# Two side loads issued later and five pieces of TensorE work put in another order, in a two-block network on one core

## The chip, the cores and the metric

The kernel runs on one core of one Trainium2 chip. The metric is the time of one execution in microseconds (us). Three runs of the kernel before took 1758.71, 1763.52 and 1771.0 us, so the median is 1763.52 us.

## The reference, cut to what matters

256 tokens of width 1024 pass through two networks one after the other, all in 32-bit floats.

```
# first network, 2 layers: mixer, then a mixture of 16 experts (each takes 32 tokens)
h = rms_norm(x) * (1 + scale) + shift            # scale, shift, gate = silu(c) @ ada_w + ada_b
layer 0 mixer: proj = h @ fc_w_in                # 1024 -> 1536: 512 Fourier, 1024 gated convolution
               y_f = real(fft2(...)); y_c = silu(layer_norm(conv31(u_v * sigmoid(u_g))))
               y = concat(y_f, y_c) @ fc_w_out
layer 1 mixer: windowed attention, 16 heads, rotary positions
x = x + gate * y;  x = x + gate * experts(...)
x = rms_norm(x, final_norm_g)

# second network, 1 layer, with 256 context tokens beside the 256 latent ones
proj_l, proj_c = hl @ w_in, hc @ w_in
a = differential attention over context and latent keys (4 heads, both 128-row blocks)
b = neighbourhood attention with a bias table rpb (4 heads)
p = pooling mix;  h = hyena mix (two long convolutions)
xl = xl + gate * (concat(a, b, p, h) @ w_out)
xl = xl + gate2 * moe(...)                       # 16 experts, top 2 inside one group
out = rmsnorm(xl, final_g)
```

## The kernel before, in words

There is one instruction stream for each engine, written out by hand in the order of execution, and semaphores between them. The two 128-token tiles (T = 0, 1) lie on the 128 partitions.

**Weights.** SyncE (SP) streams all weights in pieces of 1 MB, in the order of use, into a ring of 8 slots (`load`, line 320 on, profile line L322; pairs of pieces at L333). Before it issues piece n it waits (`place_free`) until TensorE has counted up `piece_used` far enough that the slot is free. TensorE waits in `loaded(...)` for the piece to land.

**Side loads.** GpSimd's queue (`@block.gpsimd`, L2107 on) loads small constants in a fixed order, each behind a semaphore wait. After the ninth weight piece is used it issues, without a further wait: the first gate bias (L2111), the Fourier tables (L2113), the router weights (L2114), the row constants (L2116), the first network's last gain (L2117, 512 KB in SBUF, read at L1632 of the second block's start), and four copies of the bias table from DRAM to DRAM (L2119, in rows of 127 floats; read back in `pool_block2` at L991, after the wait for `rpb_copied`). Then come the gate bias of the next site (`load_gate_bias(1)`, L2129), the filter constants, gate bias 2, `window` and `positions` (L2138, L2139), `load_gate_bias(3)`, and `pool_block2`.

**Opening.** TensorE works through the first modulation blocks (`ada_block`), the convolution half of `fc_w_in`, then the two Fourier half pieces (`P_FC_FOURIER`), the Fourier transforms, `ada_block(3..5)`, and half of the output projection. VectorE meanwhile runs the 31 taps of the convolution (L2850) and then signals `conv_ready`, for which TensorE waits before it sums the convolution over channels.

**Experts** of the first network are two loops of 16 experts (`experts`), 12 pieces each. Between them lies the attention stage (`pe_attention`): six pieces of `attn_w_qkv` (`P_QKV`), then modulation blocks 9 to 13 and the heads.

**Second mixer** (`pe_block2`, L1024 on). `context(q)` projects the context tokens with piece q of `w_in` into PSUM banks 4 and 5; after q = 3 it signals `ctx_ps`. `transposed_norm(4, 4, 0)` turns the normalised latent tokens into banks 0 to 3; VectorE and ScalarE scale them into `hT`, and TensorE waits for that in `h_ready(4)` before the latent projection. After that comes a loop over 12 head groups (8 "diff", 4 "near"; `N2` = 12). In step g TensorE does the scores of group g+1, then a block of other work chosen by g, then waits for the probabilities of group g-1, transposes them (`turned_probs`, 4 instructions, L2150), waits until ScalarE has copied them out of PSUM (`pT2_ready`), and multiplies them with the values (`weighted`). A "near" group has a second half that is transposed and copied after the first. The other work includes `keys_values(T, bank)` in steps 2 and 3 (8 rows k of the projection of keys and values, PSUM bank 5 or 7), two gate rows and four parts of the output projection (`out_part`) in steps 11 and 12.

ScalarE's own order in steps 2 and 3 is fixed in `act_block2`: first the exponentials, then a wait for `in_b_ps` and the copy of keys and values out of PSUM (L1536, L1537), then the wait for the transposed probabilities (`pT2_ps`) and their copy. GpSimd waits for `ctx_ps` before it loads the bias table (L982). A last loop of 17 experts of 6 pieces follows, and the final normalisation.

Of the kernel before, what the change touches and what calls it, by code (L numbers as in the profile page):

```python
# [29 lines left out]
P = 128  # L30
D = 1024
KD = D // P
# [32 lines left out]
P_QKV = P_ADA_8 + 4  # L65
# [122 lines left out]
def build(nc, A, WHERE):  # L188

    with ExitStack() as ctx:  # L190
# [5 lines left out]
        def S(name):  # L196

            if name not in sems:
                sems[name] = ctx.enter_context(nc.semaphore(name))
            return sems[name]  # L200
# [14 lines left out]
        rpb_rows = nc.dram_tensor("rpb_rows", (4, 7, 64, 128), F32, kind="Internal").ap()  # L215


        ps = ctx.enter_context(nc.psum_tensor("ps", [P, 8, 512], F32))
# [8 lines left out]
        rows = sb("rows", [P, width("rows")])  # L227
# [128 lines left out]
        def read(g):  # L356

            return ORDER.index(g) + 1
# [665 lines left out]
        def pe_block2(pe, mm, tr, transposed_norm, h_ready, gate_row, ada_piece, ada_block):  # L1024
# [11 lines left out]
                    last.then_inc(S("ctx_ps"), 1)  # L1036

            pe.wait_ge(S("gate_added"), 4)
            for q in range(4):
                context(q)  # L1040
            transposed_norm(4, 4, 0)
            h_ready(4)
            for T in range(NT):
                for q in range(4):
# [21 lines left out]
                if f % 2:  # L1066
                    last.then_inc(S("hy_ps"), 1)

            def keys_values(T, bank):
                for k in range(KD):  # L1070
                    last = mm(ps[:, bank, :], hT[:, k, P * T:P * T + P], wide_in(4 + k // 2)[:, k % 2, 0:512],
                              k == 0, k == KD - 1)
                last.then_inc(S("in_b_ps"), 1)

            def pool_in(bank):
                for T in range(NT):
# [47 lines left out]
            def out_part(T, i):  # L1124
                if T == 0:
                    loaded(pe, P_OUT2 + i)
                w = slot(P_OUT2 + i).rearrange("p (k f) -> p k f", k=2)
                for kk in range(2):
                    for n in range(2):
                        last = mm(ps[:, 2 * T + n, :], ycat2[:, 2 * OUT2_ORDER[i] + kk, P * T:P * T + P],  # L1130
                                  w[:, kk, 512 * n:512 * n + 512], i + kk == 0, i == 3 and kk == 1)
                if T == 1:
                    last.then_inc(S("piece_used"), 1)
                elif i == 3:
                    last.then_inc(S("out_ps"), 1)
# [73 lines left out]
            for g in range(N2 + 1):  # L1209
                if g + 1 < N2:  # L1210
                    scores(g + 1)
                if g == 0:
                    feature(2, 5)
                    feature(3, 5)
                if g == 1:
                    pe.wait_ge(S("hy_in"), 1)
                    feature(4, 7)
                if g == 2:
                    pe.wait_ge(S("hy_in"), 2)
                    keys_values(0, 5)  # L1220
                if g == 3:
                    pe.wait_ge(S("hy_in"), 3)
                    keys_values(1, 7)
                if g == 4:
                    pe.wait_ge(S("in_b_act"), 1)
                    four(5, [pla[:, T, 256 + P * i:384 + P * i] for i in range(2) for T in range(NT)])
                    pe.wait_ge(S("in_b_act"), 2)
                    pe.wait_ge(S("b2_const"), 64)
                    long_conv(0, "turn")
                if g == 5:  # L1230
                    pe.wait_ge(S("qk_ready"), 5)
                    near_keys(1, 5)
                    long_conv(0, "forward")
                if g == 6:
                    pe.wait_ge(S("y_spec"), 1)
                    pool_in(5)
                if g == 7:
                    pe.wait_ge(S("pool_m"), 16)
                    pe.wait_ge(S("in_b_dve"), 1)
                    for i in range(4):  # L1240
                        o = 64 * (i % 2)
                        for T in range(NT):
                            last = mm(ps[o:o + 64, 5, SEQ * (i // 2):SEQ * (i // 2) + SEQ], pu[:, T, 64 * i:64 * i + 64],
                                      pool_m[:, T, i, :], i < 2 and T == 0, T == NT - 1)
                    last.then_inc(S("pool_ps"), 1)
                    long_conv(1, "turn")
                if g == 8:
                    long_conv(1, "forward")
                if g == 9:
                    long_conv(1, "back")  # L1250
                if g == 10:
                    pe.wait_ge(S("oa_ready"), 1)
                    pe.wait_ge(S("hy_out"), 1)
                    for T in range(NT):
                        for i in range(2):
                            last = tr(ps[:, 7, SEQ * i + P * T:SEQ * i + P * T + P],
                                      oa[:, T].rearrange("p h d -> p (h d)")[:, P * i:P * i + P])
                    last.then_inc(S("oaT_ps"), 1)
                if g == 11:
                    pe.wait_ge(S("row_copied"), read(14))  # L1260
                    mm(ps[:, 5, :], wide[:, 1, 0, :], gate_rows[:, 4, :], True, True)
                    pe.wait_ge(S("ycat2_ready"), 1)
                    mm(ps[:, 7, :], wide[:, 1, 1, :], gate_rows[:, 4, :], True, True).then_inc(S("gate_ps"), 1)
                    pe.wait_ge(S("exps2_ready"), 22)
                    out_part(0, 0)
                    out_part(0, 1)
                if g == 12:
                    pe.wait_ge(S("o2_ready"), 10)
                    out_part(0, 2)
                    out_part(0, 3)  # L1270
                if g:
                    near_group = A_GROUPS[g - 1][0] == "near"
                    pe.wait_ge(S("probs2_ready"), g)
                    n = turned_probs(g - 1, 0)
                    if g == 1:
                        feature(5, 7)
                    if g == 4:
                        pe.wait_ge(S("qk_ready"), 4)
                        near_keys(0, 5)
                    if g == 6:  # L1280
                        long_conv(0, "back")
                    if g == 7:
                        pe.wait_ge(S("pooled"), 1)
                        for i in range(4):
                            o = 64 * (i % 2)
                            last = mm(ps[o:o + 64, 5, SEQ * (i // 2):SEQ * (i // 2) + SEQ], pool_w[o:o + 64, i // 2, :],
                                      pp[o:o + 64, i // 2, :], i < 2, True)
                        last.then_inc(S("pool_ps"), 1)
                    if g == 9:
                        ada_block(14)  # L1290
                    if g == 12:
                        pe.wait_ge(S("exps2_ready"), 24)
                        out_part(1, 0)
                        x_turned(0, (5, 7))
                    pe.wait_ge(S("pT2_ready"), n)
                    if near_group:
                        turned_probs(g - 1, 1)
                    weighted(g - 1, 0)
                    if g == 12:
                        logits(0, 5)  # L1300
                        out_part(1, 1)
                    if near_group:
                        pe.wait_ge(S("pT2_ready"), n + 1)
                        weighted(g - 1, 1)
# [803 lines left out]
        def _(pool):  # L2108
# [5 lines left out]
            pool.dma_start(routers[:, :, :, :].rearrange("p l (n t) e -> p l n t e", n=2), A["routers"].rearrange("l (n p t) e -> p l n t e", p=P, t=4))\  # L2114
                .then_inc(S("routers"), 16)
            pool.dma_start(rows[:, :], A["rows"].broadcast_to([P, rows.shape[1]])).then_inc(S("routers"), 16)  # L2116
            pool.dma_start(last_gain[:, :], A["final_norm_g"].broadcast_to([P, D])).then_inc(S("last_gain"), 16)  # L2117
            for h in range(NA_H):
                pool.dma_start(rpb_rows[h, :, :, 0:127],  # L2119
                               A["rpb"][h, 4:11].unsqueeze(1).broadcast_to([7, 64, 127]))\  # L2120
                    .then_inc(S("rpb_copied"), 16)
            ada_biases = [A["ada_b"][l, j] for l in range(2) for j in range(2)]
            gate_bias = [b[2 * D:3 * D] for b in ada_biases]
            gate_bias += [A["ada_b_2"][0, 2 * D:3 * D], A["ada_b_2"][0, 5 * D:6 * D]]
# [1 line left out]
            def load_gate_bias(k):  # L2126

                pool.wait_ge(S("x_ready"), 2 * k)
                pool.dma_start(gate[:, :], gate_bias[k].rearrange("(a f) -> a f", a=1).broadcast_to([P, D]))\  # L2129
                    .then_inc(S("gate_bias"), 16)  # L2130
# [6 lines left out]
            load_gate_bias(2)  # L2137
            pool.dma_start(window.rearrange("p a b -> p (a b)"), A["window"]).then_inc(S("phase_const"), 16)  # L2138
            pool.dma_start(posi, A["positions"]).then_inc(S("phase_const"), 16)  # L2139
            load_gate_bias(3)  # L2140
            pool_block2(pool, load_gate_bias)

# [932 lines left out]
```

## Time and profile before

| | |
|---|---|
| runs | 1758.71, 1763.52, 1771.0 us |
| median | 1763.52 us |
| profiled execution, its own time | 1758.08 us |
| its span, first to last instruction | 1756.3 us |
| granted TensorE clock, mean | 0.898 of full speed |
| busy: TensorE matmul, VectorE, ScalarE, GpSimd | 77%, 25%, 13%, 1% |
| DMA | 640 MB, mean 364 GB/s |

"L" with a number is a line of the kernel; several operations share a helper's line (all ordinary matmuls are L2147, transposes L2150, ScalarE's work L2518), so a group is told apart by its time, tiles and shape. A time is that from the start of the span. Idle time in square brackets is that of the engine just before the group, and behind the arrow is what ended it. A 32-bit matmul shows as two instructions.

### The profile page before, as it was taken

Reading aid. Unit: us, or ns where it says so; the run is one execution under the profiler, and the core shown is the slowest. Engines: PE = TensorE matmul, PEld = TensorE weight load, DVE = VectorE, ACT = ScalarE, POOL = GpSimd, SP = SyncE. Lnnn points to the kernel's source line nnn. Section 1 sums busy time; section 2 is a strip of 40 time slices with the busy share of each in tenths; the row PEclk is TensorE's granted clock in tenths of the full one; section 3 lists DMA queues with packets and bytes.
Section 4 is the critical chain, followed back from the end, with each engine's and each line's share of the span. In section 5 each row is a group of like instructions: output and inputs, shape, how many; then the busy total and the mean of one; then the engine's idle time right before and its main releaser. Section 6 shows DMA issues by size and latency. Waiting matters only on the chain.

```text
span 1756.3 us, 25665 instructions
## 1 busy us (share of the span) xinstructions
PE 1355.8 (77%) x11264; PEld 736.3 (42%) x11264; DVE 439.8 (25%) x1014; ACT 223.2 (13%) x470; POOL 25.7 (1%) x46
## 2 busy tenths in 40 slices
PE   7999665666666579897766666655699888999997
PEld 4755332332323234553323333322346645655553
DVE  1674211013100024643101000000126465322122
ACT  2122000000000021531000000000112233100001
POOL 1000000000000000000000000000020000000000
PEclk9998888888888899998788787788899999999999
DMA  9999999999999997849999999999951325899996
GB/s 375 362 367 358 427 423 427 423 426 424 426 424 426 424 407 299 343 170 399 424 425 424 426 424 427 423 426 424 419 208 65 144 109 195 345 421 421 421 420 256
DMA packets 89484, 640.11 MB, mean 364 GB/s; under 512 B 8508, under 2 KB 8508, under 8 KB 43296
## 3 DMA queue, kind: packets, MB, share of 16 engines
q1 hardware_dynamic: 85712, 625.85, 86.8%
q0 software_dynamic: 3664, 12.64, 2.0%
q8 instruction: 90, 1.47, 0.3%
q14 instruction: 18, 0.15, 0.0%
HBM read 637.40 MB, written 1.96 MB: 364 GB/s over the span
## 4 chain that ended last, share of the span: by engine, by line
DMA 48%; PE 44%; DVE 5%; ACT 1%; issue 1%; SPq 0%; DVEq 0%; ACTq 0%
PE ps L2147 42%; DMA ring<-in_moe_w_up 31%; DMA ring<-in_moe_w_down 13%; PE ps L2150 2%; DMA ring<-in_fc_w_in 2%; DMA ring<-in_attn_w_qkv 1%; DMA ring<-in_moe_w 1%; DMA ring<-in_ada_w 1%; ACT work L2518 1%; DVE work L803 0%; SPq L322 0%; DVE work L2923 0%; DVE work L784 0%; DVE work L788 0%; ACT hT L2518 0%
## 5 line engine op out<-in xcount | busy, mean ns | idle before, releaser
L2147 PE MATMUL ps<-ring,work 128*32 128x256 f32 (+3 forms) x7696 | 754.7, 457 | 330.1 <-DMA ring<-in_moe_w_gate 151.1
L2147 PEld LDWEIGHTS ps<-ring,work 128*32 128x32 f32 (+2 forms) x7696 | 349.4, 131 | 714.9 <-issue 268.7
L2518 ACT ACTIVATE work<-ps 128x256 f32<-128x256 f32 (+3 forms) x171 | 79.0, 467 | 1213.9 <-PE ps L2147 1019.3
L2957 DVE TENSOR_TENSOR work<-work,ps 128x256 f32<-128x256 f32 x32 | 13.5, 421 | 622.3 <-ACT work L2518 622.3
L2147 PE MATMUL ps<-work 32*128 32x256 f32 (+7 forms) x1098 | 155.5, 447 | 10.0 <-ACT work L2518 6.6
L2147 PEld LDWEIGHTS ps<-work 32*128 32x128 f32 (+4 forms) x1098 | 89.2, 199 | 73.7 <-issue 58.5
L2147 PE MATMUL ps<-ring,hT 128*128 128x512 f32 (+1 forms) x224 | 92.3, 573 | 6.1 <-DMA ring<-in_attn_w_qkv 3.0
L2150 PE MATMUL ps<-const,work 128*128 128x128 f32 (+1 forms) x392 | 64.0, 294 | 13.2 <-DVE work L803 6.1
L2147 PE MATMUL ps<-ring,condT 128*32 128x512 f32 x560 | 71.4, 630 | 3.0 <-DMA ring<-in_ada_w 3.0
L2147 PE MATMUL ps<-hT,ring 128*128 128x256 f32 x288 | 67.4, 395 | 4.2 <-DMA ring<-in_fc_w_in 2.6
L2147 PE MATMUL ps<-work,xn 128*128 128x128 f32 (+2 forms) x448 | 66.6, 300 | 1.8 <-DVE work L1905 1.6
L2150 PEld LDWEIGHTS ps<-const,work 128*128 128x128 f32 (+1 forms) x392 | 46.6, 161 | 48.2 <-issue 23.1
L2147 PEld LDWEIGHTS ps<-ring,hT 128*128 128x128 f32 x224 | 43.3, 195 | 54.8 <-issue 49.4
L2147 PEld LDWEIGHTS ps<-hT,ring 128*128 128x128 f32 x288 | 56.4, 198 | 16.1 <-issue 4.7
L2147 PEld LDWEIGHTS ps<-work,xn 128*128 128x128 f32 x448 | 58.1, 191 | 9.2 <-issue 7.0
L2975 DVE TENSOR_TENSOR work<-ps,gate 128x256 f32<-128x256 f32 x32 | 13.6, 425 | 153.4 <-PE ps L2147 153.4
L2850 DVE SCALAR_TENSOR_TENSOR work<-work,cols 128x256 f32<-128x256 f32 x120 | 47.6, 477 | 0.0
L2518 ACT ACT_TABLE_LOAD x28 | 35.9, 1283 | 1.8 <-DVE condT L2706 1.4
L2147 PEld LDWEIGHTS ps<-ring,condT 128*32 128x32 f32 x560 | 16.9, 115 | 43.4 <-issue 36.2
L2518 ACT ACTIVATE work<-work 128x256 f32<-128x256 f32 (+7 forms) x55 | 27.4, 500 | 47.5 <-DVE work L1735 14.5
L1967 DVE TENSOR_TENSOR work<-work,ps 128x256 f32<-128x256 f32 x17 | 7.2, 421 | 92.2 <-PE ps L2147 92.1
L2942 DVE TENSOR_SCALAR work<-ps,gain,mod 128x128 f32<-128x128 f32 x56 | 19.1, 404 | 28.1 <-PE ps L2147 28.0
(305 smaller groups left out, 655.2 us busy)
## 6 DMA issues: line engine op xcount, KB each, us to landing
ring<-in_moe_w_up SPq DMA_DIRECT2D x64, 2048.0 KB, 17.8
ring<-in_moe_w_down SPq DMA_DIRECT2D x128, 1024.0 KB, 15.9
ring<-in_moe_w_gate SPq DMA_DIRECT2D x63, 2048.0 KB, 16.9
ring<-in_moe_w SPq DMA_DIRECT2D x102, 1024.0 KB, 10.9
ring<-in_ada_w SPq DMA_DIRECT2D x70, 1024.0 KB, 10.4
ring<-in_w_in SPq DMA_DIRECT2D x10, 1024.0 KB, 18.1
ring<-in_fc_w_in SPq DMA_DIRECT2D x6, 1024.0 KB, 15.8
ring<-in_attn_w_qkv SPq DMA_DIRECT2D x6, 1024.0 KB, 20.3
```

Of the source, the lines that this page charges most:

```text
L1967: v.tensor_tensor(hid3, act3, ps[:, 5, 0:SEQ], ALU.mult).then_inc(S("hid3_ready"), 1)
L2147: return pe.matmul(out, lhsT, rhs, start=start, stop=stop, skip_group_check=True)
L2150: return pe.matmul(out, in_, ident[0:n, 0:n], is_transpose=True, start=True, stop=True, skip_group_check=True)
L2518: return nc.scalar.activation(out, in_, f, **kw)
L2850: ins = v.scalar_tensor_tensor(cv[:, g, :], src, w, cv[:, g, :], op0=ALU.mult, op1=ALU.add)
L2942: v.tensor_scalar(xe[:, c % 2, j, :], ps[:, bank, P * (j % 4):P * (j % 4) + P], gain[:, site, j:j + 1], mod[:, 3 * site, j % 4, j // 4, 0: ...
L2957: v.tensor_tensor(hid, act, ps[:, 5, 0:SEQ], ALU.mult).then_inc(S("hid_ready"), 1)
L2975: v.tensor_tensor(ye, ps[:, 7, 0:SEQ], gate[:, 0:SEQ], ALU.mult).then_inc(S("ye_ready"), 1)
```

## The change

On GpSimd's queue the load of the first network's last gain and the four copies of the bias table are issued later: behind `positions`, after a new wait for the third `attn_w_qkv` piece to be used, and ahead of `load_gate_bias(3)`. On TensorE, `context(3)` stands behind the transposes of the latent tokens; the last row k of each `keys_values` stands behind the first transposes of its step; the first of the two gate rows stands in step 10 behind the transposes, not in step 11 ahead of them; and `out_part(0, 1)` stands in step 11 behind the transposes. ScalarE's and VectorE's programs are as before.

```diff
             pe.wait_ge(S("gate_added"), 4)
-            for q in range(4):
+            for q in range(3):
                 context(q)
             transposed_norm(4, 4, 0)
+            context(3)
             h_ready(4)
...
-            def keys_values(T, bank):
-                for k in range(KD):
+            def keys_values(T, bank, rows):
+                for k in rows:
                     last = mm(ps[:, bank, :], hT[:, k, P * T:P * T + P], wide_in(4 + k // 2)[:, k % 2, 0:512],
                               k == 0, k == KD - 1)
-                last.then_inc(S("in_b_ps"), 1)
+                if rows.stop == KD:
+                    last.then_inc(S("in_b_ps"), 1)
...
                 if g == 2:
                     pe.wait_ge(S("hy_in"), 2)
-                    keys_values(0, 5)
+                    keys_values(0, 5, range(KD - 1))
                 if g == 3:
                     pe.wait_ge(S("hy_in"), 3)
-                    keys_values(1, 7)
+                    keys_values(1, 7, range(KD - 1))
...
                 if g == 11:
-                    pe.wait_ge(S("row_copied"), read(14))
-                    mm(ps[:, 5, :], wide[:, 1, 0, :], gate_rows[:, 4, :], True, True)
                     pe.wait_ge(S("ycat2_ready"), 1)
                     mm(ps[:, 7, :], wide[:, 1, 1, :], gate_rows[:, 4, :], True, True).then_inc(S("gate_ps"), 1)
                     pe.wait_ge(S("exps2_ready"), 22)
                     out_part(0, 0)
-                    out_part(0, 1)
...
                     n = turned_probs(g - 1, 0)
                     if g == 1:
                         feature(5, 7)
+                    if g in (2, 3):
+                        keys_values(g - 2, 5 if g == 2 else 7, range(KD - 1, KD))
...
                     if g == 9:
                         ada_block(14)
+                    if g == 10:
+                        pe.wait_ge(S("row_copied"), read(14))
+                        mm(ps[:, 5, :], wide[:, 1, 0, :], gate_rows[:, 4, :], True, True)
+                    if g == 11:
+                        out_part(0, 1)
...
-            pool.dma_start(last_gain[:, :], A["final_norm_g"].broadcast_to([P, D])).then_inc(S("last_gain"), 16)
-            for h in range(NA_H):
-                pool.dma_start(rpb_rows[h, :, :, 0:127],
-                               A["rpb"][h, 4:11].unsqueeze(1).broadcast_to([7, 64, 127]))\
-                    .then_inc(S("rpb_copied"), 16)
...
             pool.dma_start(posi, A["positions"]).then_inc(S("phase_const"), 16)
+            pool.wait_ge(S("piece_used"), P_QKV + 3)
+            pool.dma_start(last_gain[:, :], A["final_norm_g"].broadcast_to([P, D])).then_inc(S("last_gain"), 16)
+            for h in range(NA_H):
+                pool.dma_start(rpb_rows[h, :, :, 0:127],
+                               A["rpb"][h, 4:11].unsqueeze(1).broadcast_to([7, 64, 127]))\
+                    .then_inc(S("rpb_copied"), 16)
             load_gate_bias(3)
```

## Rows read from the trace of the kernel before

**Rows 1.** The page: chain that ended last by line, and DMA share in 40 slices.

```profile
PE ps L2147 42%; DMA ring<-in_moe_w_up 31%; DMA ring<-in_moe_w_down 13%; PE ps L2150 2%; DMA ring<-in_fc_w_in 2%; DMA ring<-in_attn_w_qkv 1%; DMA ring<-in_moe_w 1%; DMA ring<-in_ada_w 1%; ACT work L2518 1%; DVE work L803 0%; SPq L322 0%; DVE work L2923 0%; DVE work L784 0%; DVE work L788 0%; ACT hT L2518 0%
...
DMA  9999999999999997849999999999951325899996
```

**Rows 2.** Chain of waits, opening: start us, length us, what.

```profile
37.73 27.38 DMA ring<-in_fc_w_in
```

**Rows 3.** Timeline of TensorE, opening: start us, length us, group, idle before it.

```profile
24.89 8.83 PE L2147 MATMUL ps<-hT,ring 128*128 128x256 f32 x32 [1.67 <-DVE hT L2731]
...
41.62 17.51 PE L2147 MATMUL ps<-hT,ring 128*128 128x256 f32 x80
...
65.25 15.74 PE L2147 MATMUL ps<-hT,ring 128*128 128x256 f32 x64 [2.55 <-DMA ring<-in_fc_w_in]
...
113.29 1.89 PE L2147 MATMUL ps<-work,const 128*128 128x256 f32 x8
```

**Rows 4.** Stretch; its length, TensorE busy; granted clock; DMA share; GB/s.

```profile
26.00:28.00 2.00, 2.00 (x6) 0.50 1.05 386
```

**Rows 5.** Timeline of VectorE, opening: the convolution and the signal behind it.

```profile
62.92 47.59 DVE L2850 SCALAR_TENSOR_TENSOR work<-work,cols 128x256 f32<-128x256 f32 x120
110.55 0.15 DVE L2855 COPY work<-work 128x1 f32<-128x1 f32 x1
```

**Rows 6.** DMA queues from 49 to 60 us: packets, MB, share of 16 engines.

```profile
q0 software_dynamic: 715, 1.41, 41.0%
```

**Rows 7.** The page's DMA issues of the moved loads: count, KB each, us to landing.

```profile
rpb_rows<-in_rpb POOLq DMA_DIRECT2D x4, 222.2 KB, 16.5
...
last_gain<-in_final_norm_g POOLq DMA_DIRECT2D x1, 512.0 KB, 12.6
```

**Rows 8.** Timeline of TensorE, attention stage, the six query, key and value pieces.

```profile
641.73 41.44 PE L2147 MATMUL ps<-ring,hT 128*128 128x512 f32 x96 [3.05 <-DMA ring<-in_attn_w_qkv]
```

**Rows 9.** Attention stage: stretch, TensorE busy, clock, DMA share, GB/s.

```profile
662.00:667.00 5.00, 5.00 (x13) 1.00 0.94 353
667.00:685.00 18.00, 18.00 (x58) 1.00 0.51 171
```

**Rows 10.** Timeline of TensorE, start of the second mixer.

```profile
1270.24 16.21 PE L2147 MATMUL ps<-ring,work 128*128 128x512 f32 x32
1286.29 2.09 PE L2150 MATMUL ps<-const,xn 128*128 128x128 f32 x16
1290.31 27.70 PE L2147 MATMUL ps<-ring,hT 128*128 128x512 f32 x64 [1.93 <-ACT hT L2518]
```

**Rows 11.** Timeline of VectorE: last normalised tile.

```profile
1279.95 0.75 DVE L2765 TENSOR_SCALAR xn<-x,small 128x1024 f32<-128x1024 f32 x1
```

**Rows 12.** Timeline of TensorE, step 2: transposes, then the weighted values.

```profile
1353.58 0.60 PE L2150 MATMUL ps<-const,work 128*128 128x128 f32 x4
1354.92 1.10 PE L2147 MATMUL ps<-work 128*128 128x64 f32 x8 [0.75 <-ACT work L2518]
```

**Rows 13.** Chain of waits, step 2: ScalarE's two copies.

```profile
1353.78 0.45 ACT work L2518
...
1354.27 0.61 ACT work L2518
```

**Rows 14.** Timeline of TensorE, steps 10 and 11.

```profile
1429.21 0.66 PE L2150 MATMUL ps<-const,work 128*128 128x128 f32 x4 [2.66 <-ACT work L2518]
...
1431.57 1.98 PE L2147 MATMUL ps<-gate_rows,const 128*128 128x512 f32 x4
1433.39 7.03 PE L2147 MATMUL ps<-ring,work 128*128 128x512 f32 x16
...
1441.60 0.66 PE L2150 MATMUL ps<-const,work 128*128 128x128 f32 x4 [0.75 <-ACT work L2518]
```

**Rows 15.** Timeline of ScalarE, step 9: the row of modulation block 14 copied.

```profile
1421.86 0.59 ACT L2518 ACTIVATE gate_rows<-ps 128x512 f32<-128x512 f32 x1
```

**Rows 16.** Timeline of VectorE: probabilities that step 11 transposes.

```profile
1428.97 1.23 DVE L1715 TENSOR_TENSOR work<-work 128x1024 f32<-128x1024 f32 x1
```

## The prediction

> **What bounds the kernel now.** I read the chain of waits first. By line it is 44% DMA of expert weights (31 and 13) and 42% TensorE matmuls [rows 1]: the two loops of experts of the first network wait for the weight stream, and the opening, the two mixers and the attention stage wait for TensorE. The DMA share over the span says the same: full in the loops, low in the second mixer [rows 1]. Between these stages the coupling is one of order only: the stream is at most 8 pieces ahead of TensorE, so when TensorE reaches the end of a stage earlier by some amount, the slots come free that much earlier and everything behind shifts. What the change wins or loses in a stage bound by TensorE therefore reaches the end in full, unless a second chain stands close behind. Both stages that it touches are of that kind, with one exception in each: in the opening a DMA piece is late once [rows 2], and in the second mixer TensorE waits several times for VectorE or ScalarE.
>
> **Opening: what leaves.** TensorE waits 2.55 us for a Fourier piece of the input projection, which took 27.38 us from issue to landing [rows 2, 3]. Then it runs its 64 instructions in 15.74 us; at the 17.51/80 = 0.219 us that the same form takes before, they would be 14.0 us, so the wait costs 1.7 us more by the clock. The moved loads are 512 KB and 4 x 222 KB, 1.43 MB [rows 7]. On the way of the late piece GpSimd's queue moved 1.41 MB from 49 to 60 us and took 41% of 11 us, 4.5 us of all engines [rows 6]. At the plain 386 GB/s of [rows 4] these bytes would be 3.7 us. Both are more than 2.55 us, so the piece lands in time: 2.55 + 1.7 = 4.25 us gone. The five issues themselves lie on a queue that nothing waits for here.
>
> **Opening: what is late next.** The convolution on VectorE does not depend on that piece. It starts at 62.92 and its signal comes at 110.55 + 0.15 = 110.70 us [rows 5]. TensorE asks for it at 113.29 [rows 3]; 4.25 us earlier is 109.04, so it stands for 1.7 us and leaves 113.29 - 110.70 = 2.6 us earlier than before. Such a stand has a price of its own. The nearest row is an idle of 1.67 us before 24.89: the 32 instructions behind it took 8.83 us instead of 7.0 [rows 3], and from 26 to 28 us the granted clock was 0.50, the 1.2 GHz level [rows 4]. Between no loss and this 1.8 us I take 1.8, since the length of the stand is the same. Opening: -2.6 + 1.8 = -0.8 us; ends -2.6, and +0.3 if a second slow stretch of the kind falls in.
>
> **Attention stage.** The third of six pieces is used at 641.73 + 41.44/2 = 662.4 us [rows 8]; then the five loads go out. GpSimd's next duty behind them is a gate bias that waits for the end of this stage, so nothing is queued up. On the DMA engines the loads need the 4.5 us of above. From 662 to 667 the share is 0.94, from 667 to 685 it is 0.51 [rows 9]: 0.3 + 8.8 = 9.1 us of all engines stand free. TensorE works through [rows 8, 9] with slots full ahead of it. Cost 0, hidden by a stream that waits for slots; with that cover gone it would be up to 4.5 us.
>
> **context(3).** A piece of context is 8 instructions at 27.70/64 = 0.433 us, 3.5 us [rows 10]. The transposes start at 1286.3 - 3.5 = 1282.8 instead; their input is there at 1279.95 + 0.75 = 1280.7 [rows 11]. VectorE and ScalarE then finish `hT` at 1290.3 - 3.5 = 1286.8, while context(3) runs until 1288.4. The 1.93 us of idle [rows 10] go: -1.9 us, and 0 at worst. The signal `ctx_ps` comes 2.1 us later; ScalarE's copies behind it are not asked for until the heads, and GpSimd's 16 loads of the bias table are wanted in step 2, some 60 us on. Cost 0.
>
> **keys_values, twice.** TensorE does the last row (2 instructions, 0.87 us) behind the transposes, so as to fill the 0.75 us in which it waits for ScalarE [rows 12]. But look at what ScalarE does in this gap: two copies, at 1353.78 and 1354.27 [rows 13]. The first is that of the keys and values, released by the end of `keys_values`, and stands ahead of the other in ScalarE's order, which the change leaves alone. Now that projection ends 0.45 to 0.60 us later, by the four transposes put ahead of it [rows 12], and ScalarE begins both copies that much later. Everything behind follows: +0.45 us in each of the two steps, +0.9 in sum, where the gap seems to promise -0.75 each. I take the loss, since the order of ScalarE's program leaves no other way; ends -1.5 and +1.2.
>
> **Gate row.** Four instructions of two rows hold 1433.39 - 1431.57 = 1.82 us [rows 14]; one row is 0.9. In step 10 it falls into an idle of 2.66 us [rows 14]. Its input was copied at 1421.86 + 0.59 = 1422.45 [rows 15], before that idle. -0.9 us; 0 at worst.
>
> **out_part(0, 1).** Half of 7.03 us, 3.5 us [rows 14], goes behind the transposes and covers the 0.75 us until the second half's transposes may start. The transposes then start at about 1440.2 - 0.9 - 3.5 = 1435.8; the probabilities are there at 1430.2 [rows 16]. -0.75 us; 0 at worst.
>
> **Sum.** -0.8 + 0 - 1.9 + 0.9 - 0.9 - 0.75 = -3.5 us. Against the profiled execution, 1758.08 us, that is 1754.6. The median of the runs lies 5.4 us above that execution; from 1763.5 the same sum gives 1760.0 us.
>
> **Rivals.**
> - **The stand at the convolution costs no clock.** For it: how often the clock falls behind an idle of this length is not fixed, one row is little. The opening gives -2.6 and the total is -5.3: 1758.2 us.
> - **keys_values gains as it looks.** That needs ScalarE's two copies not to be the limit; [rows 13] speak against it. Then -1.5 stands for +0.9 and the total is -5.9: 1757.6 us.
> - **The opening's change doesn't do what it says.** The late piece may be late by the weight queue's own backlog, with GpSimd's share lying elsewhere; 41% in the very stretch [rows 6] speaks against. Then the opening gives 0 and the total is -2.7: 1760.8 us.
> - **The side loads collide in the attention stage (slower).** While both queues have work the side loads held 41% of the engines [rows 6], so weight pieces land later than by their bytes. It decides at 9.1 us free [rows 9] against 4.5 needed: if the pieces for modulation blocks 9 and 10 land late, TensorE waits 4.5 us right behind 683 us and loses 1.8 us by the clock: +6.3 - 3.5 = +2.8, 1766.3 us. TensorE's stream without a DMA wait there and the free share speak against it. The Trainium skill (DMA: Bandwidth & Descriptors, Queues, rings and completion order) has each engine go round between the queues that have work, whatever is urgent, and (same page, Specifications) says that transfers under 512 bytes run below line rate; the table's rows are 508 bytes. By these two the loads would press harder on the weight pieces than their bytes say, in the opening as in the new place; the trace's 41% agrees with the first.
>
> **Chances.** Forecast as summed 0.4; no clock loss 0.2; keys_values gains 0.1; no effect in the opening 0.15; collision 0.12; the rest is something not seen. The predicted time is that of the forecast, 1760. The lowest mechanism is -2.6 - 1.9 - 1.5 - 0.9 - 0.75 = -7.7, 1755.9; the highest 1766.3. The three runs before lie from 4.8 below to 7.5 above their median, and a median of new runs can move by some 3 to 5 of that by itself: range 1751 to 1769. About 1% (17.6 us) is what a measurement of this kernel can tell from no change. Every case lies inside it, so within 1% gets 0.94, and 0.03 each side.
>
> **What would show it.** Opening: no DMA wait before the Fourier instructions, and these in 14.0 us; a new idle of about 1.7 us just before the sums over channels, ended by VectorE's signal, with the clock at 0.5 behind it or not. Attention: no DMA wait from 683 on. Second mixer: no idle before the latent projection; in steps 2 and 3 an idle of more than 0.3 us left behind the last row, and 0.4 to 0.6 us more from the projection's start to the weighted values than before; step 11 about 1.7 us shorter. Wrong it would be if the loops of experts changed their pace, since I hold them to shift only, or if the wait in the opening stayed.

## The result, and the profile after

The changed kernel took 1753.81 us in the median of 20 runs (1748.86 to 1759.85), the kernel before 1761.62 in 20 runs (1750.05 to 1771.0). The ratio is 0.9961, with a 95% interval from 0.9947 to 0.9976: 6.9 us faster, between 4.2 and 9.3. The profiled execution has a span of 1747.1 us, 9.2 less than the one before.

The forecast was 1760.0 us in a range from 1751 to 1769, so the median lies inside it, and "within 1%" holds. The sum, -3.5 us, is too small: it lies just outside the interval. I had added it to 1763.5, the median of three runs; over twenty runs the kernel before takes 1761.6, so 1.9 of the 6.2 us between forecast and result are that starting point.

I read the trace of the changed kernel at the places of the rows before. First the opening, the timeline of TensorE (start us, length us, group, idle before it):

```profile
24.84 7.14 PE L2154 MATMUL ps<-hT,ring 128*128 128x256 f32 x32 [1.67 <-DVE hT L2738]
...
36.53 3.72 PE L2154 MATMUL ps<-hT,ring 128*128 128x256 f32 x16 [0.65 <-DMA ring<-in_fc_w_in]
...
61.92 14.08 PE L2154 MATMUL ps<-hT,ring 128*128 128x256 f32 x64
...
110.03 1.99 PE L2154 MATMUL ps<-work,const 128*128 128x256 f32 x8 [1.58 <-DVE work L2862]
```

Against [rows 3] the DMA wait of 2.55 us is gone, the 64 Fourier instructions take 14.08 us and not 15.74, and a new idle of 1.58 us stands where TensorE asks for the convolution. From the Fourier instructions' readiness (62.70 before, 61.92 now) to the sums over channels it is 48.11 us, where it was 50.59: 2.5 us less. The idle of 1.67 us before 24.8 is the same in both, but this time nothing is lost behind it (7.14 us, 8.83 before). That is 1.7 us by the clock, of which 0.65 us were given back at once to a DMA wait.

The loss of clock that my sum put behind this idle is not there. The clock behind the new idle (stretch; length, TensorE busy; granted clock; DMA share; GB/s):

```profile
110.03:114.00 3.97, 3.96 (x13) 1.00 1.03 410
114.00:118.00 4.00, 4.00 (x15) 1.00 0.85 339
```

The attention stage, where the side loads are now, first as GpSimd's timeline, then the queue's share from 655 to 690 us (packets, MB, share of 16 engines), then TensorE's stretches, which answer to [rows 9]:

```profile
661.05 0.53 POOL L2142 DMA_DIRECT2D last_gain<-in_final_norm_g  x1 [28.74 <-PE ps L2154]
661.61 3.24 POOL L2144 DMA_DIRECT2D rpb_rows<-in_rpb  x4
```

```profile
q1 hardware_dynamic: 2476, 9.55, 73.1%
q0 software_dynamic: 720, 1.44, 18.2%
```

```profile
660.00:665.00 5.00, 5.00 (x13) 1.00 0.94 349
665.00:683.00 18.00, 18.00 (x55) 1.00 0.85 251
```

The loads took 18.2% of 35 us, 6.4 us of all engines, and filled a stretch whose share was 0.51. TensorE works through, and up to the output's gate row it waits for no DMA, as before the change.

The second mixer. The start answers to [rows 10], steps 2 and 3 to [rows 12], step 11 to [rows 14]:

```profile
1264.99 11.31 PE L2154 MATMUL ps<-ring,work 128*128 128x512 f32 x24
1276.13 2.07 PE L2157 MATMUL ps<-const,xn 128*128 128x128 f32 x16
1278.04 3.60 PE L2154 MATMUL ps<-ring,work 128*128 128x512 f32 x8
1281.48 27.63 PE L2154 MATMUL ps<-ring,hT 128*128 128x512 f32 x64
...
1343.81 0.60 PE L2157 MATMUL ps<-const,work 128*128 128x128 f32 x4
1344.25 1.02 PE L2154 MATMUL ps<-ring,hT 128*128 128x512 f32 x2
1346.45 1.11 PE L2154 MATMUL ps<-work 128*128 128x64 f32 x8 [1.17 <-ACT work L2525]
1347.48 1.18 PE L2154 MATMUL ps<-work,gate 32*128 32x512 f32 x4
1348.59 7.88 PE L2154 MATMUL ps<-ring,hT 128*128 128x512 f32 x14
...
1418.26 1.02 PE L2154 MATMUL ps<-gate_rows,const 128*128 128x512 f32 x2
1421.11 0.66 PE L2157 MATMUL ps<-const,work 128*128 128x128 f32 x4 [1.82 <-ACT work L2525]
1421.69 1.84 PE L2154 MATMUL ps<-work 128*64 128x128 f32 x16
1423.47 1.13 PE L2154 MATMUL ps<-gate_rows,const 128*128 128x512 f32 x2
1424.43 3.60 PE L2154 MATMUL ps<-ring,work 128*128 128x512 f32 x8
1427.87 0.60 PE L2157 MATMUL ps<-const,work 128*128 128x128 f32 x4
1428.30 3.60 PE L2154 MATMUL ps<-ring,work 128*128 128x512 f32 x8
1431.74 0.60 PE L2157 MATMUL ps<-const,work 128*128 128x128 f32 x4
```

There is no idle before the latent projection. In step 2 the idle behind the moved row is longer (1.17 us) than the one it should fill (0.75). The next projection starts 0.5 us later behind the start of the one before it (10.89 us, 10.41 before) and runs part of its 14 instructions slower (7.88 us; 6.28 at full clock). The gate row sits in step 10's wait, which shrank from 2.66 to 1.82 us, and step 11 has no idle left.

### The profile page after: what moved, and what is told of

It is laid out like the page before. It is cut to its first block, busy times and chain, and to the rows that moved or that the text cites. A ratio compares the mean times of both kernels' runs of the same rounds, so it can differ in the third digit from the quotient of the medians.

```text
span 1747.1 us, 25665 instructions
## 1 busy us (share of the span) xinstructions
PE 1354.8 (78%) x11264; PEld 732.8 (42%) x11264; DVE 439.7 (25%) x1014; ACT 223.3 (13%) x470; POOL 25.7 (1%) x46
## 4 chain that ended last, share of the span: by engine, by line
DMA 47%; PE 43%; DVE 8%; ACT 1%; issue 1%; SPq 0%; DVEq 0%
PE ps L2154 41%; DMA ring<-in_moe_w_up 31%; DMA ring<-in_moe_w_down 13%; DVE work L2857 3%; PE ps L2157 2%; DMA ring<-in_attn_w_qkv 1%; DMA ring<-in_fc_w_in 1%; DMA ring<-in_ada_w 1%; ACT work L2525 1%; DVE work L803 0%; DVE work L784 0%; DVE work L788 0%; SPq L322 0%; DVE xn L1901 0%; DVE x L2824 0%
## 5 line engine op out<-in xcount | busy, mean ns | idle before, releaser
L2154 PE MATMUL ps<-ring,work 128*32 128x256 f32 (+3 forms) x7696 | 763.4, 463 | 325.8 <-DMA ring<-in_moe_w_gate 147.5
L2154 PE MATMUL ps<-work 32*128 32x256 f32 (+7 forms) x1098 | 148.7, 435 | 10.7 <-ACT work L2525 7.8
```

Source lines behind the costliest of these rows:

```text
L2154: return pe.matmul(out, lhsT, rhs, start=start, stop=stop, skip_group_check=True)
```

## The experiments

My theory: each part acts where it stands, the stages behind only shift, and the rest of the difference between the two profiles is the clock, which comes out differently from one execution to the next. Theory 2: the changed kernel gains further time in a place that my sum left at 0, above all in the attention stage, whose stretch from the first `attn_w_qkv` instruction to the output's gate row is 117.89 us after and 120.50 before. Line numbers in the rows differ by a few from kernel to kernel; the form tells the group.

**Only the side loads moved.** The kernel before with the last two hunks of the diff alone, the five loads taken out of the opening and issued here:

```diff
             pool.dma_start(posi, A["positions"]).then_inc(S("phase_const"), 16)
+            pool.wait_ge(S("piece_used"), P_QKV + 3)
+            pool.dma_start(last_gain[:, :], A["final_norm_g"].broadcast_to([P, D])).then_inc(S("last_gain"), 16)
+            for h in range(NA_H):
...
             load_gate_bias(3)
```

> The kernel before with only the five side loads moved to the attention stage. Theory 1 (each part acts where it stands, and stages behind only shift): no DMA wait before the 64 Fourier instructions, a new idle of about 1.6 us before the sums over channels, TensorE 2.6 us earlier from there; the loads cost nothing in the attention stage. Time -2.6 us against before, or -0.8 if the clock falls behind the new idle. Theory 2 (the 2.6 us that the profile of the changed kernel gains between the first attn_w_qkv instruction and the output projection come from the side loads' new place): about -5 us, and that stretch is again 117.9 us long and not 120.5. Rival (the loads collide there): a DMA wait behind the third attn_w_qkv piece and a gain of under 0.5 us.

Measured: ratio 0.9986 (0.9966 to 1.0006), 2.5 us faster with an interval from 6.0 faster to 1.1 slower. By itself that doesn't tell from no change; the trace does tell what happens:

```profile
62.66 14.08 PE L2148 MATMUL ps<-hT,ring 128*128 128x256 f32 x64
...
110.79 1.99 PE L2148 MATMUL ps<-work,const 128*128 128x256 f32 x8 [1.59 <-DVE work L2856]
```

Readiness to sums is 48.13 us again, 2.5 us less than before, and the clock behind the idle is full. The attention stretch is 117.88 us.

**Only TensorE's order changed.** The changed kernel with the loads back in the opening.

> The changed kernel with the five side loads back in the opening, so only TensorE's order is changed. Theory 1: the DMA wait of about 2.5 us before the Fourier instructions is back; the second mixer is 2.8 us shorter than before (1.9 by the context piece, 0.9 and 0.8 by gate row and output part, and 0.9 lost in steps 2 and 3). Time -2.8 us. Theory 2 gives the same here. If the excess over my sum lies in the second mixer: -5 us or more.

Measured: ratio 0.9962 (0.9941 to 0.9982), 6.7 us faster (3.2 to 10.4). The DMA wait in the opening is back (2.18 us), the attention stretch is 120.30 us. From the first context product to the latent projection it is 15.75 us, at full clock throughout, against 20.07. My -2.8 lies a little outside the interval; it fits the third case better, that what my sum lacks lies in the second mixer, and the profiles run again show below where: around the context pieces. The profiled execution is only 1.5 us shorter than the one before, since from the first context product to the last expert loop the clock stood at its half level for 27.3 us (18.2 before), worked out from the granted clock in steps of 1 us. So structure and clock pull against each other within one profile, and single spans differ by more than the effect.

**keys_values whole again.** The changed kernel without the split:

```diff
-                    keys_values(0, 5, range(KD - 1))
+                    keys_values(0, 5, range(KD))
...
-                    if g in (2, 3):
-                        keys_values(g - 2, 5 if g == 2 else 7, range(KD - 1, KD))
```

> The changed kernel with both keys_values whole and ahead of the transposes, as before. If moving the last row costs time, as ScalarE's order says, this is 0.9 us faster than the changed kernel (from projection start to weighted values 7.9 us in each of steps 2 and 3, where the changed kernel takes 8.75), and up to 1.6 us more if the clock fell behind the longer idle. If the move gains as the gap seems to promise, this is 1.5 us slower.

Measured: ratio to the kernel before 0.9957 (0.9938 to 0.9977), which doesn't tell it from the changed kernel. The trace does: from one group's weighted values to the next it is 10.31 us over step 2 and 10.41 over step 3, as in the kernel before; in the changed kernel 10.74 and 12.49. So the split costs 0.43 us in step 2, and in step 3 0.43 where the clock stays full (10.84 in the kernel with only TensorE's order changed) and 2.1 where it doesn't.

**ScalarE's copies in the other order.** The changed kernel, and in ScalarE's program:

```diff
-                if g in (2, 3):
-                    sc_.wait_ge(S("in_b_ps"), g - 1)
-                    act_(plb[:, g - 2, :], ps[:, 5 if g == 2 else 7, :], ACT.Copy).then_inc(S("in_b_act"), 1)
...
                         act_(pT2[:, 4 * b:4 * b + 4, :], ...).then_inc(S("pT2_ready"), 1)
+                if g in (2, 3):
+                    sc_.wait_ge(S("in_b_ps"), g - 1)
+                    act_(plb[:, g - 2, :], ps[:, 5 if g == 2 else 7, :], ACT.Copy).then_inc(S("in_b_act"), 1)
```

> The changed kernel with ScalarE's two copies of steps 2 and 3 in the other order: first the transposed probabilities, then the keys and values. If ScalarE's order made the moved row a loss, TensorE now fills the gap with that row: projection start to weighted values about 7.2 us in each step, against 8.75 in the changed kernel and 7.9 before: 2 x 1.5 = about 3 us faster than the changed kernel in the profile, at least 2.4. If the gap has another cause, no difference.

Measured: ratio to before 0.9952 (0.993 to 0.9975). Timeline of TensorE, steps 2 and 3:

```profile
1340.17 6.28 PE L2154 MATMUL ps<-ring,hT 128*128 128x512 f32 x14
1346.29 0.60 PE L2157 MATMUL ps<-const,work 128*128 128x128 f32 x4
1346.72 1.02 PE L2154 MATMUL ps<-ring,hT 128*128 128x512 f32 x2
1347.63 1.10 PE L2154 MATMUL ps<-work 128*128 128x64 f32 x8
...
1357.18 1.10 PE L2154 MATMUL ps<-work 128*128 128x64 f32 x8
```

The idle is gone. Projection start to weighted values is 7.46 us; it was 8.75, and 8.31 in the kernel before, where I had said 7.2 and 7.9 for the first and the last of these, but their order is as said. Weighted to weighted over both steps is 19.00 us, against 23.23 in the changed kernel and 20.71 before. This shows that ScalarE's order made the moved row a loss. The ratio against before is not clear of the changed kernel's: the interval is wider than the 2.6 to 4.2 us in question.

**The gate row of the opening ahead of the convolution's wait.** The changed kernel with

```diff
                 out_rows(0, 1)
+                gate_row(0, 0)
                 pe.wait_ge(S("conv_ready"), 1)
...
                 out_rows(1, 1)
-                gate_row(0, 0)
```

> The changed kernel with the first site's two gate-row products (four instructions, 1.8 us) done ahead of TensorE's wait for the convolution, where it now idles 1.6 us, and not behind the sums. If the convolution on VectorE is what holds the opening: the idle before the sums goes, and TensorE reaches the wait for the second half of the concatenated input 1.6 us earlier, where ScalarE's last output (about 1.1 us ahead of it so far) holds it: 1.0 to 1.1 us faster than the changed kernel. If the 1.6 us idle is not VectorE's: no difference.

Measured: ratio to before 0.9958 (0.994 to 0.9977).

```profile
110.03 1.88 PE L2154 MATMUL ps<-gate_rows,const 128*128 128x512 f32 x4
111.78 1.99 PE L2154 MATMUL ps<-work,const 128*128 128x256 f32 x8
...
126.58 5.85 PE L2154 MATMUL ps<-ring,work 128*128 128x512 f32 x13 [0.64 <-ACT work L2525]
```

The idle before the sums is filled. From the sums to the last output rows it is 14.80 us, where the changed kernel takes 15.81, and the idle of 0.64 us ended by ScalarE is the next limit: 1.0 us gained, as expected. The convolution on VectorE, and behind it ScalarE's output, bound this stretch. In the runs 1 us is not to be seen.

**Both together.**

> Both: ScalarE's two copies of steps 2 and 3 in the other order, and the gate row ahead of the convolution's wait. By the sum 3 + 1 = 4 us faster than the changed kernel where the clock is the same, about -10 us against before. If slower stretches of the clock take it back, as they did in the second mixer of the first such kernel (28.7 us at half clock where the changed kernel had 16.3), nothing or 1 to 2 us.

Measured: ratio to before 0.9948 (0.9926 to 0.9969), 9.1 us faster, between 5.4 and 13.0; the median of its 7 runs is 1749.17 us. It is the lowest ratio of all, but its interval overlaps that of the changed kernel. It keeps the local gains (19.00 us over steps 2 and 3; 14.80 us behind the sums).

**Only the gain moved**, the bias table's copies left in the opening:

> The kernel before with only the 512 KB gain moved and the four copies of the bias table left in the opening: a part of the dose. By bytes 0.52 of 1.43 MB, 1.3 to 1.6 us earlier landing, so 1.0 to 1.2 us of the 2.55 us wait before the Fourier instructions stay. If short rows cost more than their bytes, the gain's share is smaller and 1.3 us or more stay. If the side loads are not what delays the piece: 2.2 to 2.6 us stay.

```profile
63.60 14.05 PE L2148 MATMUL ps<-hT,ring 128*128 128x256 f32 x64 [1.58 <-DMA ring<-in_fc_w_in]
...
110.08 1.99 PE L2148 MATMUL ps<-work,const 128*128 128x256 f32 x8
```

**Only the table's copies moved**, the gain left in the opening:

> The kernel before with only the four copies of the bias table moved and the 512 KB gain left in the opening. By bytes 0.91 of 1.43 MB, at least 2.3 us earlier landing: 0 to 0.3 us of the wait before the Fourier instructions stay, and the idle before the sums over channels is 1.3 to 1.6 us. If the side loads are not what delays the piece: 2.2 to 2.6 us stay.

```profile
63.97 14.08 PE L2148 MATMUL ps<-hT,ring 128*128 128x256 f32 x64
...
112.09 1.99 PE L2148 MATMUL ps<-work,const 128*128 128x256 f32 x8 [1.58 <-DVE work L2856]
```

One run each, 1752.63 and 1760.7 us, which tell nothing by themselves. The dose in the traces does: with 0.52 MB away 1.58 us of the wait are left, with 0.91 MB away none. With the gain away the piece lands at 63.60 us; in the four profiles with all five loads in the opening it landed at 64.70 to 65.91, so it is 1.1 to 2.3 us earlier, where I had 1.3 to 1.6 by bytes. The wait left is longer than the 1.0 to 1.2 us that went with this, and lies where I had put the case that short rows cost more than their bytes; with a scatter of 1.2 us in the landing, one profile doesn't decide between the two. That the side loads delay the piece is shown: the wait is there in the four profiles with all five loads, and gone in the nine with the table's copies away. The first of the two has a second lesson. Its wait of 1.58 us was followed by Fourier instructions at full clock (14.05 us), and TensorE comes to the sums just when the convolution is ready, 48.06 us behind the readiness at 62.02 and with no idle. That is all that moving both gives (48.11): the rest of the earlier landing is spent standing at the convolution.

**Sixteen more copies of the table** behind the five loads in the attention stage (into a buffer that nothing reads):

```diff
+            for h in range(16):
+                pool.dma_start(rpb_again[h, :, :, 0:127], A["rpb"][h % NA_H, 4:11]...)
             load_gate_bias(3)
```

> The changed kernel with sixteen further copies of the bias table (3.6 MB, rows of 508 bytes, DRAM to DRAM, into a buffer that nothing reads) behind the five side loads in the attention stage. At the 313 GB/s at which the opening moved such loads they need 11.6 us of all DMA engines, more than the 4.6 us that my 9.1 us of free share leave behind the first five. If those 9.1 us were the limit, TensorE waits for weights by up to 7 us between blocks 9 and 13. If the eight pieces ahead of TensorE and the idle stretch further on (742 to 770 us) are the real cover, it waits nowhere and the stretch from the first attn_w_qkv instruction to the output's gate row stays 117.9 or 120.5 us.

One run, 1772.92 us, span 1771.1. The waits of TensorE from 640 to 830 us (whom for: us in total, times, longest), and the queues from 664 to 725 us:

```profile
PE ps L2159 <- DMA ring<-in_ada_w: 14.6, 6, 4.6
```

```profile
q1 hardware_dynamic: 3578, 13.80, 60.2%
q0 software_dynamic: 2880, 4.89, 40.4%
...
ring<-in_ada_w SPq DMA_DIRECT2D x13, 1024.0 KB, 22.7
```

The attention stretch is 137.70 us, 19.8 longer than in the changed kernel. Both of my numbers were too small (7 and 0). In this window GpSimd's queue moves 26% of the bytes and holds 40% of the engines' time, the pieces of `ada_w` take 22.7 us to land (9.1 in the same window of the changed kernel), and the late pieces also cost clock: granted 0.61 from 700 to 725 us, 0.93 in the changed kernel. GpSimd's own issues stop for a while too: 15 of the 20 copies go out by 675.6 us, four at 685.2 and the last at 722.9, so the gate bias behind them is late. So the place that was free for 1.44 MB is not free for 5 MB, and the idle far behind it (742 to 770 us) did not cover them.

**The same kernels again**, for the scatter:

> The kernel before, once more, for a second profile. If what the changed kernel won beyond my sum is the scatter of the clock, the attention stretch (120.5 us in the first profile) can come out at 117.9 here, and the stretch from the first context product to the latent projection (20.07 us, 4.4 us of it at half clock) can come out near 18. If it belongs to the change, both repeat within 0.2 us.

> The changed kernel once more, for a second profile. By scatter of the clock the attention stretch may be 120.5 us, the stretch from context to latent projection 15.8 to 16.7 us; the idles that I hold for structural repeat: 1.6 us before the sums, 1.17 us in steps 2 and 3, none before the latent projection.

> The kernel before, a third profile, as before_again: the attention stretch at one of the two levels 117.9 and 120.5 us by the clock, the stretch from context to latent projection between 17.6 and 20.1 us.

One run each, 1763.46, 1751.43 and 1756.15 us.

| stretch, us | before (3 profiles) | changed (2 profiles) |
|---|---|---|
| idle before the sums | 0, 0, 0 | 1.58, 1.58 |
| attn_w_qkv to output's gate row | 120.50, 120.30, 117.89 | 117.89, 117.95 |
| context to latent projection | 20.07, 18.68, 17.85 | 16.49, 16.41 |
| context to the end of the latent projection | 47.61, 47.92, 47.09 | 43.95, 43.88 |
| weighted to weighted, step 2 | 10.30, 10.30, 10.31 | 10.74, 10.73 |
| the same, step 3 | 10.41, 10.41, 10.41 | 12.49, 12.49 |
| latent projection to last expert loop | 203.63, 208.55, 205.68 | 204.22, 204.35 |
| span | 1756.3, 1761.7, 1754.4 | 1747.1, 1749.6 |

The attention stretch has two levels in the kernel before as well, so its 2.6 us do not belong to the change, and Theory 2 falls. The kernel with keys_values whole, with the loads in the new place, had 120.52. The context stretch has the clock in it too: 17.85 us is the kernel before at full clock (32 instructions in 14.00 us), and 15.76 the kernel with keys_values whole at full clock. What the order itself gives there is 2.1 us.

But this stretch ends too early to show all of it. In that very profile of the kernel before (before_third) the clock falls right behind the idle, and the latent projection takes 29.40 us, where it takes 27.63 in all eight profiles of the new order:

```profile
1287.27 29.40 PE L2147 MATMUL ps<-ring,hT 128*128 128x512 f32 x64 [1.93 <-ACT hT L2518]
```

```profile
1289.20:1291.20 2.00, 2.00 (x3) 0.50 0.75 191
```

Over the 14 profiles, from the first context product to the end of the latent projection:

| order | clock full in the context pieces | clock down in them |
|---|---|---|
| before (idle of 1.93 or 1.94 us) | 47.08, 47.09, 47.09 | 47.53, 47.61, 47.92 |
| new (no idle) | 43.22, 43.23 | 43.80, 43.87, 43.88, 43.95, 43.98, 44.18 |

The move gives 3.9 us where the context pieces ran at full clock, 3.4 to 4.1 where they did not, 3.6 by the means of all: 2.1 by the order, the rest the clock that used to fall. In the two profiles of the old order whose latent projection took 27.70 us the clock had been down in the context pieces (16.14 and 16.21 us); why it then stayed up behind the idle no run singles out.

## Why the prediction was right in kind and short in size

**Opening, the DMA wait.** Right: 2.55 us of wait and 1.7 us of clock left, the two doses show that the side loads made the piece late, and the convolution took back what was more than 2.5 us. The 2.6 us earlier were 2.5; over all profiles it is 50.22 to 51.18 us from readiness to sums with the five loads in the opening, and 48.06 to 48.13 without all or some of them.

**Opening, the price of the new stand.** Here a step failed. I put +1.8 us on it by the row of the idle before 24.89, with the reason "Between no loss and this 1.8 us I take 1.8, since the length of the stand is the same." It was 0: in all seven profiles with a stand of 1.58 or 1.59 us there the eight instructions behind it take 1.99 us, and in the one read in detail the clock is 1.00. The row that I leaned on is itself not fixed: over the 14 profiles the same idle of 1.67 us was followed by 7.14 us in three, by 8.73 to 8.83 in ten, and by 10.20 in one. The two places differ in what TensorE did before: ahead of the convolution's wait it had worked without a gap from 100.4 to 108.5 us, ahead of 24.8 it had been at short pieces (busy 1.17 of 2 us from 22 to 24). Whether that is the reason no run singles out. The first rival of my list, "no clock loss", was the right one, and the opening gave -2.5.

**Attention stage.** Cost 0 was right. Here a size was off: the loads needed 6.4 us of all engines and not 4.5, still under the 9.1 that were free. How the cover ends I learned by the sixteen copies. The Trainium skill (DMA: Bandwidth & Descriptors, Queues, rings and completion order) says that an engine goes round between queues that have work; that 40.4% went to the side loads while weight pieces waited agrees with it. The other sentence of the Trainium skill, that transfers below 512 bytes fall short of line rate (same page, Specifications), agrees in direction: 1.44 MB in 6.4 us are 225 GB/s, where the weight pieces in the same window had 373 (9.55 MB in 73.1% of 35 us). The row length alone is not the reason, since the same loads had 313 GB/s in the opening [rows 6].

**context(3).** The mechanism was right, the size was not: 2.1 us by the order where I had 1.9, and 3.6 with the clock. "The 1.93 us of idle [rows 10] go: -1.9 us" priced an idle by its length alone. On the new idle at the convolution I had put a price of clock, on the old one that goes I put none, and the runs showed the opposite of both.

**keys_values.** Right: a loss by ScalarE's order, +0.43 us in each step (+0.45 in the sum), shown by undoing the split and by turning ScalarE's order. What I left out is the clock: the idle in step 2 grew from 0.75 to 1.17 us, and in four of the five profiles with an idle of 1.17 or 1.18 us there the projection of step 3 lost some 1.5 to 1.6 us. In the seven profiles with the idle of 0.75 us it happened once. In the trace:

```profile
1346.50:1348.50 2.00, 2.00 (x12) 0.98 0.00 0
1348.50:1350.50 2.00, 2.00 (x5) 0.50 0.00 0
1350.50:1352.50 2.00, 2.00 (x5) 0.66 0.00 0
```

So this part costs 0.9 us and, most times, 1.6 more.

**Gate row and out_part(0, 1).** Right: between the weighted values of steps 10 and 11 it is 10.58 us, where it was 12.40 (12.39 in the third profile of before): -1.8, where I had -1.65.

**The sum again**, by what was measured: -2.5 + 0 - 3.6 + 0.9 - 1.8 = -7.0 us, and about -5.5 where the clock of step 3 falls. Both lie inside the interval of 4.2 to 9.3 us, and the median's -6.9 asks for nothing more. Against my -3.5, the price of the stand accounts for 1.7 us more gain, the context piece for 1.7 more, and the clock of step 3 for up to 1.5 less. The clock of step 3 stands against the other two, so part of the total's nearness is luck. The stretches outside the touched places scatter by more than any of them: the first expert loop, from the sums to `attn_w_qkv`, took from 526.6 to 531.2 us over the profiles, in no order that follows the change.

**Chances.** "Within 1%" at 0.94 was right. Between the cases the weights were off: no clock loss at the stand deserved more than half.

## What to carry to other kernels

Work that is put into a gap fills it only if what ends the gap does not wait for that work. Before moving it, look at the in-order program of the engine that ends the gap, and move that engine's step too. When a late transfer is cured, look for the next signal the engine will ask for: it caps the gain, and half the cure may be enough. An idle can be worth more than its length, by the clock behind it, so measure from well before it to well after it. For changes of under 0.5% compare short stretches at equal clock; the span of one profile scattered by 7 us here for the same kernel.

## What the runs showed of the hardware

- The same idle in the same place may or may not be followed by half clock. 1.67 us before 24.8: full clock behind it (7.14 us) in three profiles, down in eleven. 1.58 us before the sums, behind unbroken work: down in none of seven. 1.17 or 1.18 us in step 2: down in four of five. 1.93 or 1.94 us before the latent projection: down in four of six (29.40 us for 64 instructions, 27.70 in the other two).
- A wait of 1.58 us before the Fourier instructions was followed by full clock (14.05 us), those of 2.18, 2.55 and 2.60 us by half clock (15.74), and two close together (1.85 and 1.93) by more of it (16.95).
- Short DRAM-to-DRAM rows weigh on the other queue beyond their bytes. 1.44 MB of side loads (0.91 of it in such rows) took 6.4 us of all engines in the attention stage, 225 GB/s beside weight pieces at 373, and with sixteen copies more the weight pieces landed in 22.7 us and not 9.1.
